# A transformer block with product-key experts: row products and copies moved, and the second one-hot of the gates rebuilt on VectorE in both halves

## The reference

```python
qry = (t @ wq).reshape(T, PEER_HEADS, 2, PEER_DKEY // 2)
s = jnp.einsum('thcd,hcnd->thcn', qry, sub_keys)
s1, i1 = lax.top_k(s[:, :, 0], 16);  s2, i2 = lax.top_k(s[:, :, 1], 16)
cand_s = s1[..., :, None] + s2[..., None, :]          # 256 candidates of a head
top_s, top_pos = lax.top_k(cand_s, 16)                # 8 heads x 16 experts of 16384
gate = jax.nn.softmax(top_s, axis=-1)
a = gelu(einsum('ted,td->te', down[expert], t))       # down, up: 16384 x 1024
out = einsum('te,ted->td', a * gate, up[expert])
```

## Time and profile before

| | |
|---|---|
| time before, median of 3 | 1014.33 us (1013.8 to 1015.39) |
| profiled execution, its own time | 1015.79 us |
| its span in the trace | 1013.7 us |
| PE busy | 994.6 us, 98% |
| DVE busy | 821.5 us, 81% |
| ACT busy | 555.0 us, 55% |
| POOL busy | 239.8 us, 24% |
| DMA, mean | 233 GB/s |

### The profile page before, as it was taken

How to read it: one execution, slowest core, us unless ns; L and a number is a source line. 1 busy time by engine, 2 the same in 40 slices (tenths; PEclk the granted TensorE clock), 3 DMA queues, 4 the chain that set the end, 5 groups by cost and what they waited for, 6 DMA issues and landing times.

```text
span 1013.7 us, 19100 instructions
## 1 busy us (share of the span) xinstructions
PE 994.6 (98%) x7540; PEld 923.4 (91%) x7540; DVE 821.5 (81%) x1466; ACT 555.0 (55%) x969; POOL 239.8 (24%) x231
## 2 busy tenths in 40 slices
PE   9999999999999999999999999999999899999987
PEld 8988888898789999999999999999999899999974
DVE  5577766855959999977999999689989788878864
ACT  5555545455364446776666666544444367754550
POOL 3000000100057996401111111112212334223200
PEclk9999999999999999999999999999999999999999
DMA  9953334652355667887888887788888888888941
GB/s 322 372 174 99 104 106 144 205 205 93 125 166 167 197 199 221 261 268 242 270 272 284 279 267 236 268 273 280 285 295 273 284 284 311 311 302 311 339 176 41
DMA packets 67255, 235.95 MB, mean 233 GB/s; under 512 B 9184, under 2 KB 9744, under 8 KB 66784
## 3 DMA queue, kind: packets, MB, share of 16 engines
q1 hardware_dynamic: 49536, 178.28, 53.0%
q0 software_dynamic: 17056, 55.94, 16.2%
q10 hardware_dynamic: 576, 0.52, 0.2%
HBM read 224.72 MB, written 8.39 MB: 230 GB/s over the span
## 4 chain that ended last, share of the span: by engine, by line
PE 95%; DMA 2%; DVE 1%; ACT 1%; issue 1%; SPq 0%
PE psG L1615 9%; PE psG L1616 8%; PE psG L1617 8%; PE psT L1958 5%; PE psG L2017 5%; PE psT L2017 5%; PE psS L2017 5%; PE psS L1958 5%; PE psG L1958 5%; PE psO L1617 3%; PE psO L1616 3%; PE psO L1615 3%; PE psT L1960 2%; PE psG L2018 2%; PE psT L2018 2%; PE psS L2018 2%
## 5 line engine op out<-in xcount | busy, mean ns | idle before, releaser
L825 ACT ACTIVATE hi<-raw 128x1024 fp32r<-128x1024 f32 x325 | 342.4, 1057 | 185.2 <-PE psO L1617 91.8
L1076 DVE TENSOR_TENSOR lo<-raw,hi 128x1024 fp32r<-128x1024 f32 x291 | 353.7, 1219 | 56.4 <-ACT hi L825 55.9
L757 POOL TENSOR_TENSOR lo<-raw,hi 128x1024 fp32r<-128x1024 f32 x34 | 84.4, 2489 | 99.3 <-ACT hi L825 98.8
L1615 PE MATMUL psG<-b_two,hi 128*128 128x224 f32 (+1 forms) x352 | 98.6, 280 | 0.4 <-ACT hg_t L853 0.4
L1616 PE MATMUL psG<-b_two,hi 128*128 128x224 f32 (+1 forms) x352 | 97.1, 276 | 0.0
L1617 PE MATMUL psG<-b_two,lo 128*128 128x224 f32 (+1 forms) x352 | 97.1, 276 | 0.0
L1593 DVE TENSOR_TENSOR act_two<-H,act_two 128x224 fp32r<-128x224 f32 x128 | 49.1, 387 | 49.6 <-ACT act_two L1058 49.1
L2017 PE MATMUL psG<-act_two,hi 128*128 128x448 f32 x240 | 85.1, 384 | 0.0
L2017 PE MATMUL psS<-act_two,hi 128*128 128x448 f32 x240 | 82.9, 376 | 0.3 <-DVE lo L1076 0.3
L2017 PE MATMUL psT<-act_two,hi 128*128 128x448 f32 x240 | 83.1, 376 | 0.0
L1958 PE MATMUL psT<-b_two,hi 128*128 128x448 f32 x240 | 77.2, 378 | 0.0
(11 more groups left out here) (400 smaller groups left out, 2812.2 us busy)
## 6 DMA issues: line engine op xcount, KB each, us to landing
raw<-in_down SPq DMA_DIRECT2D x128, 512.0 KB, 4.4
raw<-in_up SPq DMA_DIRECT2D x128, 512.0 KB, 4.9
raw<-in_w_stream SPq DMA_DIRECT2D x73, 512.0 KB, 3.7
one_kept<-one POOLq DMA_DIRECT2D x28, 256.0 KB, 4.8
one<-one_kept POOLq DMA_DIRECT2D x28, 256.0 KB, 5.1
w<-in_w SPq DMA_DIRECT2D x4, 512.0 KB, 11.7
xT<-in_xT SPq DMA_DIRECT2D x4, 256.0 KB, 5.2
memT<-in_memT SPq DMA_DIRECT2D x1, 1024.0 KB, 6.1
```

The lines of the kernel that those rows point to most:

```text
L757: pool.tensor_tensor(lo[slot(n)][:], raw[slot(n)][:], hi[hi_slot(n)][:].bitcast(FP32), ALU.subtract)\
L825: act.activation(hi[hi_slot(n)][:], raw[slot(n)][:], ACT.Copy).then_inc(hi_done, 1)
L1076: dve.tensor_tensor(lo[slot(n)][:], raw[slot(n)][:], hi[hi_slot(n)][:].bitcast(FP32), ALU.subtract)\
L1615: pe.matmul(out, hi_l, hi_r, start=start, stop=False)
```

## The change

Three things. `save_one2` and `load_one2` and their DRAM tensor go; `one_hot` makes `one2` for all 56 groups. The 32 products stand at new positions: 16 at 44 to 74 (one in two), 10 at 78 to 114 (one in four), 6 at u61 to u71 (one in two); before it was 16 at 42 to 117 and 16 at u58 to u84. The 32 raises: 8 at u5 to u54 (one in seven), 8 at u62 to u76 (one in two), 16 at u79 to u116 (one in 2.5); before 16 at u5 to u57 and 16 at u91 to u116. From u61 to u72 every position therefore has a use of a row. For this there are three `x_apart` tensors, filled before the table, at position 58 and at u57 (before: at u52), and `apart_w` is filled at position 62 instead of 44.

```diff
-DOT_AT = [42 + 75 * q // (SPAN - 1) for q in range(SPAN)] + [E_TILES + 58 + 7 * q // 4 for q in range(SPAN)]
-RAISE_AT = [E_TILES + 5 + 7 * q // 2 for q in range(SPAN)] + [E_TILES + 91 + 27 * q // 16 for q in range(SPAN)]
+DOT_AT = ([44 + 2 * q for q in range(SPAN)] + [78 + 4 * q for q in range(10)]
+          + [E_TILES + 61 + 2 * q for q in range(6)])
+RAISE_AT = ([E_TILES + 5 + 7 * q for q in range(8)] + [E_TILES + 62 + 2 * q for q in range(8)]
+            + [E_TILES + 79 + 5 * q // 2 for q in range(SPAN)])
-X_AT = E_TILES + 52
+X_USE = [0] * SPAN + [1] * 10 + [2] * 6
+X_AT, WEIGHTS_AT = (E_TILES + 57, 58), 62
-    if at == X_AT:
-        out.append(("copy_x", 1))
+    if at in X_AT:
+        out.append(("copy_x", 2 - X_AT.index(at)))
+    if at == WEIGHTS_AT:
+        out.append(("weights", 0))
-        x_apart = [sb(f"x_apart{i}", [P, D], at=R_at + (213, 80)[i] * 512) for i in range(SETS)]
+        x_apart = [sb(f"x_apart{i}", [P, D], at=R_at + (152, 213, 80)[i] * 512) for i in range(3)]
-                    save_one2(0)
-                elif what == "gates" and j + 1 < GROUPS:
-                    save_one2(j + 1)
-                elif what == "gates" and j + 1 < 2 * GROUPS:
-                    load_one2(j + 1)
-                if half == 0:
-                    if g >= 2:
-                        dve.wait_ge(one2_out[s], 16 * (g // 2))
-                    dve.tensor_tensor(one2[s][:], columns(0, NK), pairs(i2T, NK), ALU.is_equal)
+                dve.tensor_tensor(one2[s][:], columns(0, NK), pairs(i2T, NK), ALU.is_equal)
                 if g >= GROUPS:
-                    pe.wait_ge(one2_back[s], 16 * ((g - GROUPS) // 2 + 1))
                     pe.wait_ge(gated, g)
```

More of the change, by code:

```diff
@@ L651, in build @@
         expert_in, apart_w_in = sem("expert_in"), sem("apart_w_in")
-        apart_x_in = [sem(f"apart_x_in{i}") for i in range(SETS)]
+        apart_x_in = [sem(f"apart_x_in{i}") for i in range(3)]
         chunk_done, fold_low, fold_copy, folded = sem("chunk_done"), sem("fold_low"), sem("fold_copy"), sem("folded")
-        one2_out = [sem(f"one2_out{i}") for i in range(2)]
-        one2_back = [sem(f"one2_back{i}") for i in range(2)]
         rows_in = [sem(f"rows_in{i}") for i in range(ROWS)]
@@ L760, in copy_x @@
             def copy_x(i):
-                own = slice(P - APART + i * SPAN, P - APART + (i + 1) * SPAN)
+                first = P - APART + min(i, SETS - 1) * SPAN
+                own = slice(first, first + SPAN)
                 for h in range(PH):
                     pool.dma_start(x_apart[i][h * SPAN:(h + 1) * SPAN, :], x2[own, NT - 1, :]).then_inc(apart_x_in[i], 16)
[L765 to L776, removed]
             pool.wait_ge(shifted, 1)
@@ L796, in _ @@
                 elif what == "copy_x":
-                    pool.wait_ge(act_lo, X_H)
+                    if j == 2:
+                        pool.wait_ge(act_lo, X_H)
                     copy_x(j)
-                elif what == "index":
+                elif what == "weights":
                     pool.wait_ge(gate_ready, 1)
@@ L1515, in product @@
                 dve.wait_ge(rows_in[r % ROWS], 16 * (r // ROWS + 1))
-                if k % SPAN == 0:
-                    dve.wait_ge(apart_x_in[k // SPAN], 16 * PH)
-                dve.tensor_tensor(rows[r % ROWS][:], rows[r % ROWS][:], x_apart[k // SPAN][:], ALU.mult)\
+                if k == X_USE.index(X_USE[k]):
+                    dve.wait_ge(apart_x_in[X_USE[k]], 16 * PH)
+                dve.tensor_tensor(rows[r % ROWS][:], rows[r % ROWS][:], x_apart[X_USE[k]][:], ALU.mult)\
                     .then_inc(products, 1)
@@ L2137 @@
            for k, v in arrays.items()}
-    aps["one2"] = nc.dram_tensor("one2_kept", (GROUPS, P, TOK * NK), F16, kind="Internal").ap()
     aps["out"] = nc.dram_tensor("out_x", (S, D), FP32, kind="ExternalOutput").ap()
```

## The result

The changed kernel took 1030.07 us (median of 4 runs, 1028.25 to 1030.38), the kernel before, run beside it, 1014.86 us (1013.8 to 1017.15). The ratio is 1.015, 95% interval 1.0132 to 1.0169: slower by 1.5%. The forecast was 1013.3 us with a range of 1008.3 to 1018.5, so it was wrong, and on the side of the rival "the row buffers become the bound", which was itself put too low. The profiled execution has a span of 1027.7 us against 1013.7.

The account below looks back on a forecast made before the run. It took TensorE's own pace plus its waits and low-clock stretches as the bound. Terms of -4.4, 0, +1.5, +5.9 and -4.0 sum to -1.0 us, from the median 1014.33 to 1013.3 us; range 1008.3 to 1018.5.

Parts of the forecast that it names:

- the row buffers become the bound: At u61 to u72, long landings overrun the three buffers' turn; 1018.1 us, at worst 1022.1; chance 0.17.
- The load of one2, -4.4: At the u55 gate product, the 2.7 us wait and its 1.7 us of low clock go: -4.4 us.
- one2 on VectorE, 0: In the second half, 28 more VectorE operations hide in its 15.5 us of waiting for act_two: 0 us.
- 16 products by 74, 26 by 114, +1.5: In the down gates, denser products use up VectorE's lead and make TensorE late: +1.5 us, between 0.5 and 3.
- The lead is allowed to grow with it: Later down gates: added products grow to five, VectorE's lead grows too, so the cost stays 1.2 us.
- Twelve positions with a use each, +5.9: At u61 to u72, three buffers' turns exceed three tiles, so VectorE and then TensorE wait: +5.9 us.
- landing 7.1: At u61 to u72, each gather was taken to land in 7.1 us, between 7.6 among products and 6.6 among raises.
- The waits would be pieces of about 1.5 us: At u61 to u72, TensorE's waits come in pieces too short to lower the clock: no clock loss added.
- The end, -4.0: Before the last eight tiles, earlier gathers save 2.3 us of wait and 1.7 of low clock: -4.0 us.
- Quick gathers: At u61 to u72, landings near 5.8 us make the cost 1.6 instead of 5.9: 1009.0 us; chance 0.22.
- The load's place is taken: At the gates near u55, TensorE waits for the longer one_hot instead, in small pieces: 1016.0 us; chance 0.07.
- The end stays: Before the last eight tiles, folding still waits for u123, so the 4.0 us do not come: 1017.3 us; chance 0.11.

Follow-up runs that it names:

- run 1: Kernel before with only one2 rebuilt on VectorE in both halves, all products, raises and copies unmoved; 1009.19 us, ratio 0.9968.
- the probe: Kernel before with VectorE work that computes nothing, of four kinds in turn, beside each gather of u5 to u57; 1047.91 us.
- run 5: Changed kernel with the copy of position 58 issued before the table; 1026.61 us, ratio 1.0131.
- run 12: Changed kernel: position 58's copy before the table, even down products, u61 to u76 uses spread, a gap after each; 1014.97 us, ratio 1.0001.
- the sparse one: Kernel before with one2 on VectorE, three x_apart, products at new thinner positions, last 16 raises at u86 to u116; 1009.94 us, ratio 0.9956.
- run 6: Changed kernel with its first 26 products spread evenly over down 44 to 114; 1027.6 us, one execution.
- run 2: Changed kernel with the uses of u61 to u76 spread to one in 1.75 positions, last 16 raises at old places; 1022.15 us, ratio 1.0071.
- run 4: Changed kernel with the 14 gathers for u61 to u76 fetching half rows, VectorE's work unchanged; 1027.05 us, one execution.
- run 9: Changed kernel with VectorE waiting for the end of its own product or raise at u61 to u76; 1023.43 us, ratio 1.0108.
- run 3: Changed kernel with products and raises of u61 to u76 working on 64 of 1024 columns, gathers unchanged; 1019.69 us, one execution.
- run 7: Changed kernel with apart_w back at position 44; 1030.6 us, one execution.

## Why the prediction was wrong, point by point

**The load of one2, -4.4: right** (run 1). **one2 on VectorE, 0: right** (run 1, and the ledger from 650 to 800 us reads 1.9 in every kernel but the probe).

**16 products by 74, 26 by 114, +1.5: wrong, it was +7.4.** Two steps failed. (a) I had looked at `copy_x` only for what is queued behind it on GpSimd, and wrote that "the third gather now comes earlier beside the stream; I add 0.3". Its copies land beside the stream and made tiles late, and with a product in every second position beside them that cost 3.8 us (run 5), low clock included. The late tile had stood in the trace before: one asked for at 793.96, beside the `copy_x` of 792.52, took 7.8 us to land, the one ahead of it 4.2. That it costs nothing by itself is seen there as well: run 1 keeps that copy and loses 0.2 us, and so does run 12, where tiles beside the copy of u57 took up to 9.6 us to land. (b) "The lead is allowed to grow with it ... I take the same 1.2." It did not grow. Between 66 and 121 the kernel before has 11 products and loses nothing, the sparse one has 10 and loses nothing; the changed one has 15 and loses 3.6 once the copy is out (run 5); even steps have 17 and lose 5.1 (run 6) and 5.2 (run 12). That is 0.9 us for each product above eleven, near the 1.14 us that one takes: with VectorE busy for 43.63 of 44 us, the lead hides little of an added product. These counts are from the runs; no run varied them alone.

**Twelve positions with a use each, +5.9: right place, wrong term and wrong size, it was +13.3** (9.6 to 13.8 over the executions). Followed along the buffers, my turn for u66 ended with "landing 7.1". The landing was 9.9 and 10.3 us, of which 5.2 and 5.5 were the issue held by VectorE. I had the row with 1.88 us and read it as a constant of the gather; the kernel before has another price too (timeline of GpSimd, before):

```profile
449.25 0.94 POOL L793 DMA_INDIRECT rows<-in_down_rows,expert  x1 [11.56 <-PE psG L1960]
```

Two prices for one instruction were the hint. With a gap behind each use the crowd cost 7.2, against my 5.9. The other 6 us are the held issues and the clock. "The waits would be pieces of about 1.5 us ... so I add no clock" failed with it: a held issue makes VectorE idle for 5.5 us at once, so the waits come in pieces of 4.9 and 3.8 us, with two clock drops that cost 4.4 us. Nor was the premise safe: in runs 2 and 4 waits of 1.71 to 1.76 us were followed by a low clock. The loop feeds itself: VectorE behind has no gaps, so its gathers are held, so it waits, and is behind.

**The end, -4.0: it was -2.9, but most of it not by the step that I gave.** Run 1, with every raise in its old place, has 0.4 us less wait and 1.7 us less low clock, so at most the last 1.1 us of wait can be the moved raises' (2.5 to 1.4), and 0.5 of that stands again in a wait just before u118, which run 1 does not have (0.3 in the kernel before). What the earlier gathers do shows when each kernel's `hi` of u123 starts, against the end of TensorE's last product before the wait. Before: 0.0 us ahead of it, with the last gather 16.2 us ahead, wait 2.97. One2 alone: 0.4 ahead, gather 16.2, wait 2.53. Run 2, old raise positions: 2.3, 18.0, wait 1.40. Sparse: 3.4, 22.7, 1.40. Changed: 3.6, 23.2, 1.41. So u123 does come in time with them, but it did in run 2 as well, where a wait of 0.8 us before u118 had given it part of its lead. Below 1.4 us the wait is copy and fold themselves, which I had not counted: 0.7 us of my 2.3. Why the clock stayed high behind run 1's 2.53 us is open.

**The rivals.** "The row buffers become the bound" was the right one in place, with a landing of 8.2 us as its point of decision; the cause of the long landings was not in it. At its worst it had 1022.1. "Quick gathers" is what remains when issues are free, in part (7.2 us of lateness, not 1.6). "The load's place is taken" is false at u55. "The end stays" is false too. The chance of 0.17 for the rival rested on landings "up to 9.0 as it stands", as if the change could not lengthen them.

## What to carry to other kernels

Before packing work onto an engine, look at what its gaps were doing for the others: here a gather issued by GpSimd needs a pause in VectorE's work, and a schedule that leaves none holds the transfers on which VectorE itself will wait. When the same instruction shows two durations in a trace (0.94 and 1.88 us), find out what stands beside each before using either as a price. A stage in which an engine is busy for 99% takes added work at nearly full price, whatever lead it seems to have, and a bulk copy makes the tiles beside it late, so it is to be placed where the engines behind them have slack, not only where its queue is free.

## What was not expected of the hardware

- The time of a gather's issue on GpSimd: 0.94 us beside an idle VectorE, mostly 1.0 to 1.9 us beside a busy one, up to 6.94 us (run 2). Where it was over 1.0 us, it ended 0.79 to 0.90 us behind the end of a VectorE operation on SBUF operands, and never passed one that had a gap behind it (33 ns were enough).
- A wait added to the busiest helper engine made the kernel faster: run 9 against the changed kernel, 1.0108 against 1.0150 of the kernel before (the intervals overlap a little; the ledger's crowd went from 13.4 to 7.2).
- The length of TensorE's wait did not decide alone whether the clock fell. Waits of 2.35 us (run 2, near 478 us), 2.53 us (run 1, before the last tiles) and 2.89 us (run 3, near 483 us) left the granted clock at 1.00; one of 2.26 us (run 7, near 477 us) was followed by 0.54, and waits of 1.75 us (run 2, 868.7 us) and 1.76 us (run 4, 484.5 us) by a stretch at 0.5. The windows of runs 2 and 7:

```profile
478.50:481.90 3.40, 3.40 (x25) 3.23 (x23) 2.94 (x6) 1.96 (x5) 3.10 (x5) 1.00 0.10 19
```

```profile
477.90:481.30 3.40, 3.40 (x18) 3.17 (x16) 2.94 (x6) 1.61 (x4) 0.94 (x1) 0.54 0.71 231
```

- Eight copies of 64 KB between places in SBUF made a 512 KB tile of the stream come about 10 us after its issue (457.26 to 467.31 us; its landing itself is not in that trace). In run 7, with the same copies, such tiles landed 9.8 and 9.9 us after their issue, in the kernel before at that place 4.0 to 5.0.
